# A decoder trunk's feed-forward down stage in seven block products, with the differences on GpSimd

## The chip, the cores and the metric

The kernel runs on one core of a Trainium2 chip. The metric is the device time of one execution in microseconds (us), lower is better; the runs are given by their median. A core has TensorE (PE in the profile), VectorE (DVE), ScalarE (ACT), GpSimd (POOL) and SyncE (SP), which issues most of the transfers here.

## The reference

Two layers of a decoder trunk over 512 tokens of width 1024, all in float32. Each layer has two feed-forward half-steps, one around a token mixer and one after a cross-attention to 256 memory tokens:

```python
def swiglu(x, w_gu, w_down):
    g, u = jnp.split(x @ w_gu, 2, axis=-1)
    return (jax.nn.silu(g) * u) @ w_down

for layer in range(DEPTH):                     # 2
    f = swiglu(rmsnorm(h, g[0]), ffn_w_gu[layer, 0], ffn_w_down[layer, 0])
    h = h + 0.5 * rmsnorm(f, g[1])
    m = mixer(rmsnorm(h, g[2]))                # even: sparse attention and RG-LRU; odd: gated linear attention
    h = h + rmsnorm(m, g[3])
    c = mem_cross_attention(rmsnorm(h, g[4]), rmsnorm(mem, g[6]), ...)
    h = h + rmsnorm(c, g[5])
    f = swiglu(rmsnorm(h, g[7]), ffn_w_gu[layer, 1], ffn_w_down[layer, 1])
    h = h + 0.5 * rmsnorm(f, g[8])
```

The hidden width of the feed-forward parts is 2816, so `w_down` is 2816 x 1024: 22 blocks of 128 rows (k-tiles). The down product is (512 x 2816) times (2816 x 1024), four times in the program.

## The kernel before

**Precision.** Every large product is made of three matmuls. A float32 operand is split into a high part (`ACT.Copy` on ScalarE into the type fp32r, `split_hi`) and the rest (a subtraction on VectorE, `split_lo`); the product sums high x high, high x low and low x high.

**Weights.** All weights stand in memory as one stream of units of 128 x 1024 elements (512 KB). SyncE loads each unit into a raw buffer (`w_raw`, two places; `w_raw_odd`, two more in the feed-forward parts), ScalarE and VectorE split it into one of four slots (`w_hi`, `w_lo`), and TensorE reads it. SyncE waits for the split of the unit that had the raw place before (`w_ready`), ScalarE for the last matmul on the slot (`w_free`). `AHEAD` is 4: in the loop over units, ScalarE and VectorE split unit q + 4 when unit q is done.

**The feed-forward part.** `ffn` has two stages. Gate-up makes 22 hidden tiles of 128 features by 512 tokens; the first two plainly, the other 20 each by a seven-product scheme (`seven`) on blocks of 256 tokens, with its weight sums on VectorE. One such pair of gate and up tiles takes 84 matmuls of 256 columns; ScalarE and VectorE fill `act_raw`, the product of silu(gate) and up. The down stage (`output(i, "down", 11, ...)`) is plain: for each half of the 1024 output columns (`hf`), eleven units of two k-tiles by 512 columns; for each unit, four token tiles `t` accumulate in four banks of PSUM. The activation tiles are stationary (128 x 128), the weights move (512 columns). In the first half, ScalarE and VectorE also split the activations, two k-tiles at a time (`act_upper`, `act_lower`), into `act_hi` and `act_lo`. The last three units of the second half are kept in places of their own and run tile by tile, so that the norms of finished token tiles begin while TensorE works.

**Around it.** `post_square` on ScalarE squares and sums each finished tile from PSUM, `store_half` on VectorE multiplies it by the gain into `f`, `post` and `update` scale it and add it to the residual `h`. Then `norm` scales `h` into `f`, TensorE transposes it (`turn_x`), and ScalarE and VectorE split the transposed tile into `x_hi` and `x_lo`. Each engine runs its list in the written order; semaphores order the engines among each other. GpSimd has work in the even mixer (part 1: a convolution, part of the RG-LRU, six weight splits) and some masks; in the feed-forward parts it has none.

## Time and profile before

| what | value |
|---|---|
| median of 3 runs | 2197.55 us (2197.55 to 2197.93) |
| profiled execution | span 2196.3 us, 1.25 us under the median |
| TensorE busy | 2181.2 us, 99% |
| VectorE busy | 1456.1 us, 66% |
| ScalarE busy | 1127.0 us, 51% |
| GpSimd busy | 110.4 us, 5% |
| mean granted TensorE clock | 0.999 |

The profile is of one execution, by the hardware profiler. The span runs from the first instruction to the last; what the runs' times have beyond it lies around the program. Matmuls are pipelined, so their recorded durations overlap, and the distance from one start to the next is the cost of one. A granted clock of 1.00 is the full 2.4 GHz.

### The profile page before, as it was taken

To read this page: it belongs to the slowest core of one execution; us is meant where nothing else is said; L and a number is where in the kernel's file an instruction comes from. 1 tells how busy PE (TensorE), PEld (TensorE's weight loads), DVE (VectorE), ACT (ScalarE), POOL (GpSimd) and SP (SyncE) were. 2 spreads that over 40 slices of the span, in tenths; PEclk is the share of its full clock that TensorE was granted. 3 is DMA by queue.
4 is the path that set the end of the run, shared out by engine and by line. 5 is a ranking of instruction groups with operands and counts; after the bars stand their busy time and mean duration, and the time that the engine had idled before them with its cause. 6 is when DMAs were issued, how large, how long until landed. Compare 5 with 4: busy or idle time off the path is not lost.

```text
span 2196.3 us, 36637 instructions
## 1 busy us (share of the span) xinstructions
PE 2181.2 (99%) x13844; PEld 1944.0 (89%) x13844; DVE 1456.1 (66%) x2185; ACT 1127.0 (51%) x1881; POOL 110.4 (5%) x104
## 2 busy tenths in 40 slices
PE   9999999999999999999999999999999999999999
PEld 8999888775888899998899998887868889999987
DVE  8888636788666598874388885345266656888732
ACT  6555524476554565563365554245345546555531
POOL 0000000675000000000000000000000000000000
PEclk9999999999999999999999999999999999999999
DMA  4332332221452233332323323322214422333322
GB/s 164 105 105 95 115 106 63 77 77 49 144 165 79 74 115 105 105 105 96 115 87 105 105 95 115 115 81 87 96 36 138 155 79 77 103 105 105 110 99 78
DMA packets 61953, 221.44 MB, mean 101 GB/s; under 512 B 7953, under 2 KB 8081, under 8 KB 61858
## 3 DMA queue, kind: packets, MB, share of 16 engines
q1 hardware_dynamic: 57456, 208.69, 28.9%
q10 hardware_dynamic: 4402, 11.46, 1.5%
q8 instruction: 62, 1.02, 0.2%
q14 instruction: 33, 0.27, 0.0%
HBM read 218.03 MB, written 2.10 MB: 100 GB/s over the span
## 4 chain that ended last, share of the span: by engine, by line
PE 93%; DVE 4%; ACT 1%; POOL 1%; issue 1%; DMA 0%; DVEq 0%; POOLq 0%
PE ps L2099 12%; PE ps L2100 12%; PE ps L2101 12%; PE ps L2195 11%; PE ps L2197 11%; PE ps L2196 11%; PE ps L479 6%; PE ps L480 6%; PE ps L481 6%; PE ps L2035 1%; DVE e_sc L1768 1%; DVE e_max L1767 1%; DVE e_sc L1783 1%; PE ps L2583 0%; PE ps L2560 0%
## 5 line engine op out<-in xcount | busy, mean ns | idle before, releaser
L417 DVE TENSOR_TENSOR w_lo<-w_raw,w_hi 128x1024 fp32r<-128x1024 f32 x204 | 252.5, 1241 | 358.2 <-ACT w_hi L412 357.3
L412 ACT ACTIVATE w_hi<-w_raw 128x1024 fp32r<-128x1024 f32 x210 | 221.6, 1057 | 311.4 <-PE ps L2197 225.4
L2099 PE MATMUL ps<-t_hi,w_hi 128*128 128x256 f32 x1280 | 362.3, 283 | 0.0
L2100 PE MATMUL ps<-t_lo,w_hi 128*128 128x256 f32 x1280 | 362.2, 283 | 0.0
L2101 PE MATMUL ps<-t_hi,w_lo 128*128 128x256 f32 x1280 | 362.2, 283 | 0.0
L2099 PE MATMUL ps<-x_hi,w_hi 128*128 128x256 f32 x960 | 271.7, 283 | 0.0
L2100 PE MATMUL ps<-x_lo,w_hi 128*128 128x256 f32 x960 | 271.7, 283 | 0.0
L2101 PE MATMUL ps<-x_hi,w_lo 128*128 128x256 f32 x960 | 271.7, 283 | 0.0
L1490 DVE TENSOR_TENSOR w_lo<-f,w_hi 128x1024 fp32r<-128x1024 f32 x152 | 186.2, 1225 | 124.0 <-ACT w_hi L840 124.0
L479 PE MATMUL ps<-x_hi,w_hi 128*128 128x256 f32 (+1 forms) x736 | 250.8, 341 | 1.6 <-DVE x_lo L1367 0.9
L480 PE MATMUL ps<-x_lo,w_hi 128*128 128x256 f32 (+1 forms) x736 | 246.0, 334 | 0.0
L481 PE MATMUL ps<-x_hi,w_lo 128*128 128x256 f32 (+1 forms) x736 | 245.8, 334 | 0.0
L2100 PEld LDWEIGHTS ps<-t_lo,w_hi 128*128 128x128 f32 x1280 | 245.7, 192 | 0.0
L2101 PEld LDWEIGHTS ps<-t_hi,w_lo 128*128 128x128 f32 x1280 | 245.7, 192 | 0.0
L2099 PEld LDWEIGHTS ps<-t_hi,w_hi 128*128 128x128 f32 x1280 | 245.7, 192 | 0.0
L2195 PE MATMUL ps<-w_hi,act_hi 128*128 128x512 f32 x608 | 236.6, 389 | 0.0
L2196 PE MATMUL ps<-w_lo,act_hi 128*128 128x512 f32 x608 | 236.6, 389 | 0.0
L2197 PE MATMUL ps<-w_hi,act_lo 128*128 128x512 f32 x608 | 236.5, 389 | 0.0
L853 ACT ACTIVATE tmp<-ps 128x256 f32<-128x256 f32 x320 | 123.1, 385 | 173.9 <-PE ps L2101 171.1
L840 ACT ACTIVATE w_hi<-f 128x1024 fp32r<-128x1024 f32 x152 | 160.4, 1055 | 85.2 <-PE ps L2101 84.4
L2099 PEld LDWEIGHTS ps<-x_hi,w_hi 128*128 128x128 f32 x960 | 184.3, 192 | 0.0
L2100 PEld LDWEIGHTS ps<-x_lo,w_hi 128*128 128x128 f32 x960 | 184.3, 192 | 0.0
(352 smaller groups left out, 4317.8 us busy)
## 6 DMA issues: line engine op xcount, KB each, us to landing
w_raw<-in_wstream SPq DMA_DIRECT2D x310, 512.0 KB, 3.3
w_raw_odd<-in_wstream SPq DMA_DIRECT2D x80, 512.0 KB, 3.3
tmp<-in_post_gains ACTq DMA_DIRECT2D x8, 512.0 KB, 5.1
gain_bc<-in_gains ACTq DMA_DIRECT2D x7, 512.0 KB, 3.8
h<-in_x SPq DMA_DIRECT2D x4, 512.0 KB, 5.7
c_mem<-in_mem ACTq DMA_DIRECT2D x2, 1024.0 KB, 5.8
out_dram<-h SPq DMA_DIRECT2D x3, 512.0 KB, 2.7
c_gain<-in_mem_gains ACTq DMA_DIRECT2D x2, 512.0 KB, 7.5
```

The lines of the kernel that those rows point to most:

```text
L412: nc.scalar.activation(weights(v)[0], raw(v), ACT.Copy).then_inc(w_hi_ready, 1)
L417: nc.vector.tensor_tensor(wl, raw(v), wh.bitcast(f32), ALU.subtract).then_inc(w_ready, 1)
L479: nc.tensor.matmul(dst, wh, xh, start=start, stop=False)
L480: nc.tensor.matmul(dst, wh, xl, start=False, stop=False)
L481: return nc.tensor.matmul(dst, wl, xh, start=False, stop=stop)
L1490: nc.vector.tensor_tensor(wl, S[:, n * UW:(n + 1) * UW], wh.bitcast(f32), ALU.subtract)\
L2099: nc.tensor.matmul(dst, wh[:, at], xh[:, b, :], start=first, stop=False, skip_group_check=True)
L2100: nc.tensor.matmul(dst, wh[:, at], xl[:, b, :], start=False, stop=False, skip_group_check=True)
L2101: last = nc.tensor.matmul(dst, wl[:, at], xh[:, b, :], start=False, stop=final, skip_group_check=True)
L2195: nc.tensor.matmul(dst, ah, wh, start=start, stop=False)
L2196: nc.tensor.matmul(dst, ah, wl, start=False, stop=False)
L2197: return nc.tensor.matmul(dst, al, wh, start=False, stop=stop)
```

## The change

The down stage becomes a seven-product scheme on 2 x 2 blocks. The hidden features are cut in even and odd k-tiles (11 each), the tokens in two halves of 256, the output columns in two halves of 512. Each product takes one block of activations (or a sum of blocks), 11 k-tiles by 256 tokens, and one block of weights (or a sum), 11 k-tiles by 512 columns. A product is run in six steps (`PU`): five of two k-tiles and one of one k-tile; a step is 12 matmuls (the last 6) over two token tiles. There are 42 steps and 42 weight units in a part, where there were 22.

The products run in turn: `LOW_2`, `LOW_1`, `SUM_1`, `SUM_2`, `LOW_3`, `SUM_3`, `SUM_4`. `LOW_` products take a weight block as it is, `SUM_` products a running difference of weight blocks, made on GpSimd (`block_sum`) in place over the block kept since `LOW_1` (in the space of `x_hi` and `x_lo`), or over the raw buffer. The sums of activation blocks (`s3_sum` in gate-up; `second`, `first`, `third` in down) are on GpSimd as well, and two of the gain multiplies (`gained`). ScalarE and VectorE split each step's operand (`op_upper`, `op_lower`, 512 elements) into a ring of nine places and each step's weights as before. ScalarE copies a finished product's banks to `f` where they are needed twice (`keep_tiles`), VectorE adds the other product to it (`down_add`), and `down_square` squares from `f`. Post and update of token tiles 0 and 1, and the scaling of the next norm for them, are placed inside the last product; tiles 2 and 3 follow after it. The last two units are run tile by tile, with the next part's transpositions between.

```diff
+QT = FT // 2
+PU = -(-QT // 2)
+PRODUCTS = 7
+LOW_2, LOW_1, SUM_1, SUM_2, LOW_3, SUM_3, SUM_4 = range(PRODUCTS)
+BLOCK = (1, 0, 2, 3, 3, 0, 1)
+RING = 9
...
-    "ffn": [("gate_up", 2 * FT), ("down", FT)],
+    "ffn": [("gate_up", 2 * FT), ("down", PRODUCTS * PU)],
...
         def split_hi(act, v):
-            act.wait_ge(w_in[RAW[v]], RAW_COUNT[v] * 16)
+            if v in DOWN and DOWN[v][1] in SUMMED:
+                act.wait_ge(down_sum, sum_count(v))
+            else:
+                act.wait_ge(w_in[RAW[v]], RAW_COUNT[v] * 16)
...
+            def ffn(i):
+                n0, s0, d0 = nffn[i] * FT, SEVENS[i], U[i, "down"]
+                q0, r0 = 3 * PU * nffn[i], len(SUMMED) * PU * nffn[i]
+                for k in range(QT):
+                    pool.wait_ge(gu_free, n0 + 2 * k + 3)
+                    place = by_half[:, 0, 1, k, :]
+                    nc.gpsimd.tensor_tensor(place, by_half[:, 0, 0, k, :], place, ALU.subtract).then_inc(s3_sum, 1)
+                def second(m):
+                    pool.wait_ge(gu_free, n0 + 2 * (2 * m + TILES[m] - 1) + 4)
+                    pool.wait_ge(s3_sum, QT * nffn[i] + 2 * m + TILES[m])
+                    nc.gpsimd.tensor_tensor(operand(SUM_2, m), operand(SUM_4, m), operand(SUM_3, m), ALU.subtract)\
+                        .then_inc(op_sum, 1)
+                def first(m):
+                    pool.wait_ge(op_sum, q0 + 2 * m + 1)
+                    pool.wait_ge(op_ready, PRODUCTS * PU * nffn[i] + PU * LOW_1 + m + 1)
+                    nc.gpsimd.tensor_tensor(operand(SUM_1, m), operand(SUM_2, m), operand(LOW_1, m), ALU.add)\
+                        .then_inc(op_sum, 1)
+                def third(m):
+                    pool.wait_ge(op_ready, PRODUCTS * PU * nffn[i] + PU * LOW_2 + m + 1)
+                    nc.gpsimd.tensor_tensor(operand(LOW_3, m), operand(LOW_2, m), operand(SUM_2, m), ALU.subtract)\
+                        .then_inc(op_sum, 1)
+                def block_sum(p, m):
+                    v = d0 + PU * p + m
+                    pool.wait_ge(w_in[RAW[v]], RAW_COUNT[v] * 16)
+                    if p == SUM_3:
+                        pool.wait_ge(down_sum, r0 + PU + m + 1)
+                        nc.gpsimd.tensor_tensor(raw(v), block_place(m), raw(v), ALU.subtract).then_inc(down_sum, 1)
+                    else:
+                        pool.wait_ge(w_ready, d0 + PU * {SUM_1: LOW_1, SUM_2: SUM_1, SUM_4: SUM_2}[p] + m + 1)
+                        if p == SUM_4:
+                            pool.wait_ge(down_sum, r0 + 2 * PU + m + 1)
+                        nc.gpsimd.tensor_tensor(block_place(m), raw(v), block_place(m), ALU.subtract)\
+                            .then_inc(down_sum, 1)
+                def gained(o):
+                    pool.wait_ge(o_sq, square_count(i, o, 1))
+                    pool.wait_ge(post_in, 16 * (i + 1))
+                    place = f[:, 0:2, o * SEQ:(o + 1) * SEQ]
+                    nc.gpsimd.tensor_tensor(place, place, tmp[:, 2 + o:3 + o, :].to_broadcast([P, 2, SEQ]), ALU.mult)\
+                        .then_inc(down_gain, 1)
+                pool.wait_ge(prod, 5 * (s0 + FT))
+                for m in range(PU):
+                    second(m)
+                    first(m)
+                for m in range(PU):
+                    block_sum(SUM_1, m)
+                for m in range(PU):
+                    block_sum(SUM_2, m)
+                for m in range(PU):
+                    third(m)
+                gained(0)
+                for m in range(PU):
+                    block_sum(SUM_3, m)
+                gained(1)
+                for m in range(PU):
+                    block_sum(SUM_4, m)
...
+            def down(i):                                  # ScalarE
...
+                for c in range(last):
+                    if d0 + c + AHEAD < NU:
+                        split_hi(act, d0 + c + AHEAD)
+                    while ahead <= min(c + 6, 2 * c + 5, last - 1):
+                        op_upper(i, ahead)
+                        ahead += 1
...
+                    if c == PU * LOW_3 + PU + 1:
+                        down_square(i, 1, 0)
+                        down_square(i, 1, 1)
...
+            def down(i):                                  # VectorE
+                for c in range(last):
+                    if d0 + c + AHEAD < NU:
+                        split_lo(dve, d0 + c + AHEAD)
+                    while ahead <= min(c + 6, 2 * c + 5, last - 1):
+                        op_lower(i, ahead)
+                        ahead += 1
...
+                    if c == PU * SUM_4:
+                        down_add(i, 0, 2)
+                        down_add(i, 0, 3)
+                        post(i + 1, 0)
+                        update(i + 1, 0)
...
+            def down(i):                                  # TensorE
+                first_bank = (2, 0, 4, 0, 4, 0, 2)
+                def tiles(c, t, final):
+                    p, m = divmod(c, PU)
+                    pe.wait_ge(w_ready, d0 + c + 1)
+                    pe.wait_ge(op_ready, PRODUCTS * PU * nffn[i] + c + 1)
...
+                            nc.tensor.matmul(dst, ah, wh, start=start, stop=False, skip_group_check=True)
+                            nc.tensor.matmul(dst, ah, wl, start=False, stop=False, skip_group_check=True)
+                            last = nc.tensor.matmul(dst, al, wh, start=False, stop=stop, skip_group_check=True)
```

The engine names in comments are added here. Step c of a part is weight unit c of its 42.

## Rows read from the trace of the kernel before

**Rows 1.** The page: engines, and the chain that ended last.

```profile
PE 2181.2 (99%) x13844; PEld 1944.0 (89%) x13844; DVE 1456.1 (66%) x2185; ACT 1127.0 (51%) x1881; POOL 110.4 (5%) x104
...
PE 93%; DVE 4%; ACT 1%; POOL 1%; issue 1%; DMA 0%; DVEq 0%; POOLq 0%
```

**Rows 2.** Windows, the first down stage: stretch, its length, busy time by engine.

```profile
core 0: us, PE busy (x) PEld busy (x) DVE busy (x) ACT busy (x) POOL busy (x), PEclk, DMA share, GB/s
239.50:359.10 119.60, 119.42 (x532) 98.64 (x530) 52.23 (x61) 44.35 (x59) 0.00 (x0) 1.00 0.35 114
```

**Rows 3.** TensorE's timeline in down, 24 matmuls apart: start, duration, instruction.

```profile
246.35 0.39 PE L2195 MATMUL ps<-w_hi,act_hi 128*128 128x512 f32 x1
...
251.79 0.39 PE L2195 MATMUL ps<-w_hi,act_hi 128*128 128x512 f32 x1
```

**Rows 4.** VectorE's timeline in down and after it.

```profile
251.78 1.23 DVE L417 TENSOR_TENSOR w_lo<-w_raw,w_hi 128x1024 fp32r<-128x1024 f32 x1 [3.08 <-ACT w_hi L412]
252.92 1.22 DVE L1598 TENSOR_TENSOR act_lo<-act_raw,act_hi 128x1024 fp32r<-128x1024 f32 x1
...
349.16 1.29 DVE L1338 SCALAR_TENSOR_TENSOR h<-f,stat,h 128x1024 f32<-128x1024 f32 x1
```

**Rows 5.** ScalarE's timeline in down.

```profile
250.69 1.06 ACT L412 ACTIVATE w_hi<-w_raw 128x1024 fp32r<-128x1024 f32 x1 [3.43 <-PE ps L2197]
251.65 1.04 ACT L913 ACTIVATE act_hi<-act_raw 128x1024 fp32r<-128x1024 f32 x1
...
295.50 0.60 ACT L692 ACTIVATE tmp<-ps 128x512 f32<-128x512 f32 x1 [0.24 <-PE ps L2197]
296.00 0.19 ACT L692 ACTIVATION_READ_ACCUMULATOR tmp<-ps 128x1 f32 x1
```

**Rows 6.** GpSimd's timeline in the even mixer.

```profile
439.85 2.36 POOL L614 TENSOR_TENSOR w_lo<-w_raw,w_hi 128x1024 fp32r<-128x1024 f32 x1
...
495.91 1.33 POOL L629 TENSOR_TENSOR tmp<-tmp,e_t 128x512 f32<-128x512 f32 x1
...
506.00 1.30 POOL L647 TENSOR_TENSOR tmp<-e_bd,tmp 128x512 f32<-128x512 f32 x1
507.38 2.15 POOL L648 TENSOR_TENSOR e_xc<-tmp,e_xc 128x512 f32<-128x512 f32 x1
...
516.43 1.30 POOL L647 TENSOR_TENSOR tmp<-gain_bc,tmp 128x512 f32<-128x512 f32 x1
```

**Rows 7.** VectorE's timeline in the same stretch.

```profile
496.13 2.18 DVE L417 TENSOR_TENSOR w_lo<-w_raw,w_hi 128x1024 fp32r<-128x1024 f32 x1
...
506.34 2.04 DVE L417 TENSOR_TENSOR w_lo<-w_raw,w_hi 128x1024 fp32r<-128x1024 f32 x1
508.30 1.77 DVE L1834 SCALAR_TENSOR_TENSOR e_gate<-e_t,e_gate 128x512 f32<-128x512 f32 x1
...
516.72 0.69 DVE L1817 TENSOR_TENSOR x_lo<-ps,x_hi 128x512 fp32r<-128x512 f32 x1 [1.72 <-ACT x_hi L1157]
```

**Rows 8.** TensorE's timeline where the next part's first projection starts.

```profile
361.23 0.39 PE L2197 MATMUL ps<-w_late,act_lo 128*128 128x512 f32 x1
361.46 0.28 PE L479 MATMUL ps<-x_hi,w_hi 128*128 128x256 f32 x1
```

**Rows 9.** VectorE's timeline in the last gate-up pairs; TensorE's matmuls start 0.12 us apart.

```profile
226.68 1.22 DVE L1490 TENSOR_TENSOR w_lo<-f,w_hi 128x1024 fp32r<-128x1024 f32 x1 [0.97 <-ACT w_hi L840]
...
229.29 1.23 DVE L1490 TENSOR_TENSOR w_lo<-f,w_hi 128x1024 fp32r<-128x1024 f32 x1 [0.67 <-ACT w_hi L840]
230.43 0.68 DVE L1496 TENSOR_TENSOR w_lo<-w_raw_odd,w_hi 128x512 fp32r<-128x512 f32 x1
```

**Rows 10.** TensorE's timeline at the end of gate-up: products three and seven of a pair begin.

```profile
232.32 0.28 PE L2099 MATMUL ps<-t_hi,w_hi 128*128 128x256 f32 x1
...
238.08 0.28 PE L2099 MATMUL ps<-t_hi,w_hi 128*128 128x256 f32 x1
```

**Rows 11.** DMA issues: size, median time from issue to landing.

```profile
w_raw<-in_wstream SPq DMA_DIRECT2D x310, 512.0 KB, 3.3
```

**Rows 12.** Windows around the one fall of the clock, and in the odd mixer.

```profile
520.00:524.00 4.00, 2.50 (x10) 1.35 (x10) 3.96 (x6) 4.00 (x9) 3.32 (x4) 1.00 0.00 0
524.00:528.00 4.00, 3.09 (x12) 1.34 (x12) 4.00 (x8) 2.43 (x7) 2.17 (x3) 0.78 0.01 2
...
1600.00:1620.00 20.00, 20.00 (x108) 9.62 (x107) 14.10 (x39) 7.52 (x30) 0.00 (x0) 1.00 0.00 1
```

More of the change, by code:

```diff
@@ L67, in trunk @@
     ALU, ACT, AX = mybir.AluOpType, mybir.ActivationFunctionType, mybir.AxisListType
-    U, _ = unit_starts(parts)
-    NU = wstream.shape[0]
+    U, NU = unit_starts(parts)
     NP = len(parts)
@@ L193, in bank @@
             return ps[:, b, :]
-        w_in = [sem(f"w_in{n}") for n in range(4)]
+        w_in = [sem(f"w_in{n}") for n in range(4 + PU)]
         w_hi_ready = sem("w_hi_ready")
@@ L297, in trunk @@
                         continue
-                    late = q - (k - late_units(i)) if seg in ("down", "out") else -1
+                    if seg == "down" and q >= PRODUCTS * PU - 2:
+                        SLOT.append(SLOTS + q - (PRODUCTS * PU - 2))
+                        LAST_USE.append(u - PU)
+                        continue
+                    late = q - (k - late_units(i)) if seg == "out" else -1
                     if kind == "cross" and seg == "out" and q == k // 2:
@@ L325, in trunk, with width, block_place, unit_source @@
                     RAW_COUNT.append(raw_count[s])
-        def raw(u):
-            return w_raw[:, RAW[u], :] if RAW[u] < 2 else w_raw_odd[:, RAW[u] - 2, :]
+        DOWN = {U[i, "down"] + n: (i, n // PU, n % PU) for i, (kind, _, _) in enumerate(parts) if kind == "ffn"
+                for n in range(PRODUCTS * PU)}
+        TILES = (2,) * (PU - 1) + (QT - 2 * (PU - 1),)
+        def width(u):
+            return TILES[DOWN[u][2]] * SEQ if u in DOWN else UW
+        def raw(u):
+            if RAW[u] >= 4:
+                return block_place(DOWN[u][2])
+            return w_raw[:, RAW[u], 0:width(u)] if RAW[u] < 2 else w_raw_odd[:, RAW[u] - 2, 0:width(u)]
+        def block_place(m):
+            return d_t[:, 2 * m:2 * m + TILES[m], :].rearrange("p a b -> p (a b)")
+        def unit_source(u):
+            return block_place(DOWN[u][2]) if u in DOWN and DOWN[u][1] in (SUM_1, SUM_2, SUM_4) else raw(u)
         def feeds_selection(i):
@@ L354, in trunk, with square_count, half_count, full_count @@
         nffn = [sum(k == "ffn" for k, _, _ in parts[:i]) for i in range(NP)]
+        def square_count(i, o, t):
+            if parts[i][0] == "ffn":
+                return TT * 2 * i + (2 * o + t if t < 2 else 2 + 2 * o + t) + 1
+            return TT * 2 * i + TT * o + t + 1
+        def half_count(i, t):
+            before = sum(2 if parts[k][0] == "ffn" else 1 for k in range(i) if not feeds_selection(k + 1))
+            return before + (2 if parts[i][0] == "ffn" and t >= 2 else 1)
+        def full_count(i, hf, t):
+            return sum(2 * (TT - 1) for k, _, _ in parts[:i] if k != "ffn") + (TT - 1) * hf + t + 1
+        def down_cols(o, t):
+            hf = o if t < 2 else 1 - o
+            return slice(hf * SEQ, (hf + 1) * SEQ)
         ncross = [sum(k == "cross" for k, _, _ in parts[:i]) for i in range(NP)]
@@ L705, in post_mean @@
                 else:
-                    act.wait_ge(half_ssq, sum(not feeds_selection(k) for k in range(1, i + 1)))
-                    act.wait_ge(o_sq, TT * (2 * i - 1) + t + 1)
+                    act.wait_ge(half_ssq, half_count(i - 1, t))
+                    act.wait_ge(o_sq, square_count(i - 1, 1, t))
                     bias = stat[:, i, t:t + 1]
@@ L787, in norm @@
                     whole(1)
+                    whole(2)
+                    upper(3)
+                    whole(3)
+                elif parts[i - 1][0] == "ffn":
+                    down_square(i - 1, 1, 2)
+                    post_mean(i, 2)
+                    down_square(i - 1, 1, 3)
+                    post_mean(i, 3)
+                    whole(0)
+                    square(2)
+                    whole(1, (0,))
+                    square(3)
+                    whole(1, (1,))
+                    upper(2)
                     whole(2)
@@ new lines, in ffn, with op_upper @@
+                down(i)
+            def op_upper(i, c):
+                p, m = divmod(c, PU)
+                if p == LOW_2:
+                    act.wait_ge(gu_free, nffn[i] * FT + 2 * (2 * m + TILES[m] - 1) + 4)
+                elif p in (SUM_1, SUM_2, LOW_3):
+                    done = {SUM_1: 2 * m + 2, SUM_2: 2 * m + 1, LOW_3: 2 * PU + m + 1}[p]
+                    act.wait_ge(op_sum, 3 * PU * nffn[i] + done)
+                elif p == SUM_3:
+                    act.wait_ge(s3_sum, QT * nffn[i] + 2 * m + TILES[m])
+                if c >= RING:
+                    act.wait_ge(w_free, U[i, "down"] + c - RING + 3)
+                nc.scalar.activation(list(operand_place(c))[0], operand(p, m), ACT.Copy).then_inc(op_hi, 1)
@@ L1294, in _ @@
                     gla(i)
-            for t in range(TT):
-                post(NP, t)
+            for t in range(2, TT):
+                down_square(NP - 1, 1, t)
+                post_mean(NP, t)
         @block.vector
@@ L1415, in norm @@
                     return lower
+                elif parts[i - 1][0] == "ffn":
+                    down_add(i - 1, 1, 2)
+                    down_add(i - 1, 1, 3)
+                    post(i, 2)
+                    update(i, 2)
+                    post(i, 3)
+                    update(i, 3)
+                    scale(2)
+                    scale(3)
+                    lower(2)
+                    lower(3)
                 else:
@@ L1434, in last_update @@
             def last_update():
[L1435 to L1437 removed]
+                down_add(NP - 1, 1, 2)
+                down_add(NP - 1, 1, 3)
+                post(NP, 2)
+                update(NP, 2)
                 post(NP, TT - 1)
```

357 lines of the change are left out of this document (261 added, 96 removed).

## The prediction

> **What bounds the kernel now.** The page comes first. TensorE is busy for 99% of the span, and the chain that ended last is 93% TensorE [rows 1]. So only two things can shorten this kernel, fewer or shorter matmuls, and anything can lengthen it that leaves TensorE without operands. Next I read the down stage as a stretch. Between 239.5 and 359.1 TensorE is never starved, VectorE is busy 52.2 of 119.6 us, ScalarE 44.4, GpSimd not at all [rows 2]. TensorE's own timeline gives the cadence: the 24 matmuls of one unit start at 246.35 and those of the next at 251.79, so 5.44 us a unit, 0.2267 us a matmul of 512 columns [rows 3]. The recorded 389 ns are longer than the spacing because matmuls overlap; only the spacing counts. Four feed-forward parts of 22 units make 4 x 119.7 = 479 us. In each unit ScalarE and VectorE split one weight unit and, in the first half, one activation unit: VectorE 1.14 us and ScalarE 0.96 us from start to start for 1024 elements [rows 4, 5].
>
> **What is removed.** Seven products of 11 k-tiles by 2 row tiles, three matmuls each, are 462 matmuls in place of 22 x 8 x 3 = 528. 66 x 0.2267 = 15.0 us less per part, 59.8 us in all; the stage would take 104.7 us. The shape (128x128 stationary, 512 moving) stays, so the cadence stays. That is all the gain there is.
>
> **What is added on VectorE and ScalarE.** A step is now 12 matmuls, 2.72 us, 42 steps a part (35 of two tiles, 7 of one). Each step needs a weight split (1024 elements) and an operand split (512). VectorE: 35 x (1.14 + 0.60) + 7 x (0.60 + 0.34) = 67.5 us; six adds from PSUM (0.6 each), two updates, one gain multiply and two scalings (1.14 to 1.2 each) bring it to about 77 us. ScalarE: 35 x (0.96 + 0.50) + 7 x 0.8 = 57 us and the squares, 0.8 each [rows 4, 5]. Both are under 104.7 us, so neither engine alone would be the bound.
>
> **What is added on GpSimd.** In gate-up eleven differences of 256 elements; in down 18 operand sums (15 of 512 elements, 3 of 256), 24 weight sums (20 of 1024, 4 of 512), two gain multiplies of 1024. Free of VectorE, GpSimd's rows show 2.36 us for 1024 elements and 1.30 for 512 [rows 6]; 256 would be some 0.75 by the same slope. 15 x 1.30 + 3 x 0.75 + 20 x 2.36 + 4 x 1.30 + 2 x 2.36 = 78.9 us. Alone that too fits in 104.7 us.
>
> **Where they do not fit together.** The mixer before has the one stretch where GpSimd and VectorE work side by side, and the two timelines read together are the centre of this forecast [rows 6, 7]. GpSimd starts a 512-element product at 506.00 and ends at 507.30. VectorE starts a weight split at 506.34; it takes 2.04 us in place of 1.22 and ends at 508.38, so its data moved for only 1.07 us, from the moment GpSimd ended. GpSimd's next op starts at 507.38 and takes 2.15 us, that is 1.15 us after 508.38, ending at 509.53. VectorE's next starts at 508.30 and ends at 510.07, 0.54 us after 509.53. At 495.91 and 496.13 the same again (2.18 us). They alternate, strictly, with nothing overlapped. At 516.72 VectorE reads PSUM and SBUF beside a running GpSimd op and takes its normal 0.69: only ops with two SBUF inputs are held. So there is one shared passage, and I sum the time each op holds it: VectorE 1.07 for 1024 elements, 0.54 and 0.27 below; GpSimd 1.15 for 512, 0.6 for 256, and 2.23 for 1024 (between twice 1.15 and 2.36 less the same start-up of 0.15).
>
> The Trainium skill (SBUF — State Buffer, section Who interferes with whom) says the same of a Vector instruction with two SBUF inputs against a GpSimd instruction that reads SBUF, and exempts one with at most one SBUF input. By that rule the six adds from PSUM stay out of the sum; were they in, it would be 3.2 us a part larger. By that rule, the trace agrees.
>
> The holds of one part:
> VectorE, weight splits 35 x 1.07 + 7 x 0.54 = 41.2; operand splits 35 x 0.54 + 7 x 0.27 = 20.8; updates, gain multiply, scalings 5 x 1.07 = 5.4. Together 67.4 us.
> GpSimd, operand sums 15 x 1.15 + 3 x 0.6 = 19.1; weight sums 20 x 2.23 + 4 x 1.15 = 49.2; gain multiplies 4.5. Together 72.8 us.
> Sum 140.2 us, against 104.7 us of matmuls. A full step on a weight sum holds 2.23 + 1.07 + 0.54 = 3.84 us where TensorE takes 2.72: in four of seven products TensorE waits 1.1 us in every step. Before, nothing of GpSimd was in this stage, and VectorE's own 43 us of splits were hidden.
>
> **What is not saturated.** (a) GpSimd is let go at about 238.0, after product five of the last pair, but its second op waits for operand 6, which VectorE makes in loop 1, behind ScalarE's wait for step 1 (239.5 + 5.4). Some 3.4 of those 9 us are lost. (b) Before product SUM_4, GpSimd multiplies the second gain; that waits for two squares, which ScalarE issues after step 31, behind its split of unit 35. Queued behind it on GpSimd is every weight sum of the last product, and behind those ScalarE's split_hi(36) and TensorE. I take 2 us of idle passage; TensorE itself stands some 6 us there. (c) After the last scaling come a transposition and nine matmuls, 0.8 + 2.0 us. From 238.0: 140.2 + 3.4 + 2 + 2.9 = 148.5, so the stage ends at 386.5. Before, the next projection starts at 361.46 [rows 8]. That is +25 us. With the ops' whole durations in place of their holds (VectorE 73, GpSimd 78.9, sum 152) it is +37 us. The rows showed holds, but 44 GpSimd ops and their semaphores will not always follow at once; I take +28, nearer the holds.
>
> The last part has no next norm (two scalings, four splits, two transpositions: 8 us less against 2.3 less before), so +22. 3 x 28 + 22 = +106 us.
>
> **Edits at nothing.** The eleven gate-up differences hold the passage 0.6 us once in two pairs, 20 us. The two sums' splits end at 227.91 and 230.52, and TensorE first reads them at 232.3 and, 24 matmuls of 0.12 us later, 235.2; the last split ends at 231.11 and is read at 238.08 [rows 9, 10]. 4 us of slack cover 0.6; without it the four parts' 44 cost 44 x 0.6 = 26 us. Weight DMA rises from 22 to 38.5 units of 512 KB a part, about 135 GB/s in place of 114 [rows 2]; a load lands in 3.3 us [rows 11], and the loop split, load, sum, split, split is 3.3 + 2.36 + 1.06 + 1.22 us plus waits of at most 3.3, 11.2 us for four units, 2.8 a step, under 3.84. If its waits double, it is 4.4 a step: 22 steps x 0.56 = +12 us a part, the upper end. The norms after the stage lose about a microsecond, since two tiles are scaled inside it as before; gain 0 to 1 us a part, taken as nothing.
>
> **The sum.** Against the profiled span 2196.3: 2302. The runs' median lies 1.25 us above the span, so 2303.5.
>
> **Rivals.**
> Other side: the passage does not bind, because GpSimd runs in gaps that VectorE leaves anyway. For it: each engine alone fits (77 and 79 of 104.7 us). Then the stage shrinks by 15 us less the stand before SUM_4, about 3: 4 x -12 = -48, 2150 us. Against it: every overlap in the mixer was stretched. It decides from the point where holds sum to under 105 us a part; I count 140. 8%.
> The loop through DMA and GpSimd binds instead: +12 a part, 2350. 10%.
> The clock: in 524 to 528, after a stretch in which TensorE was busy 2.5 of 4 us, the granted clock was 0.78, partly its lower level of 1.2 GHz; in 1600 to 1620 it stayed at 1.00 through 108 small matmuls [rows 12]. If it stayed at 1.2 GHz through a stage, a step is 5.44 us, TensorE is the bound again, and 462 matmuls take 209 us: +80 to 90 a part, 2540. I expect it to fall only at the two stands (before SUM_1 and SUM_4), where TensorE then is slower than 3.84 for a step or two and catches up: 0 to 3 us, inside the range. 4%.
> The Trainium skill (TensorE: Matmul & The Clock Gate, Part 1) has the clock at half after idleness and full again after sustained work; that rule, too, would bring it back within the product.
>
> **How the numbers follow.** Forecast 76%, loop 10%, no binding 8%, clock 4%, gain eaten to within 0.2% 2%. Holds alone without (a) and (b) give +20 x 3 + 14 = +74, 2271; whole durations give +142, 2340; the loop 2350. I widen the lower end to 2250, since VectorE's holds may partly fall where GpSimd waits on a semaphore, and take 2250 to 2355. 0.2% of this kernel, 4.4 us, is what a measurement can tell. Faster 8%, same 2%, slower 90%.
>
> **What would show it.** In the changed profile: 1848 down matmuls at 0.227 us; a weight sum on GpSimd of 2.4 us alone and above 3 beside VectorE; operand splits on VectorE of 0.6 stretched to 1.5 to 3; TensorE's waits in down put to VectorE's and ScalarE's splits, most in the four summed products; down stages of about 147 us. The forecast is wrong if VectorE's splits keep 1.22 and 0.68 us, if the stage is under 120 us, or if the clock in it reads well under 1.

## The result, and the profile after it

The changed kernel took 2328.78 us (median; 2328.68 to 2329.37), the kernel before on the same chip 2197.55 us (2197.43 to 2197.93). The ratio is 1.0597, with a 95% interval of 1.0582 to 1.0612: 131.2 us slower. The forecast was 2303.5, +106, with a range of 2250 to 2355. The profiled execution spans 2327.1 us, 130.8 more than before.

From the page of the changed kernel, the lines that answer to [rows 1], and two groups of GpSimd's:

```profile
PE 2179.5 (94%) x13580; PEld 1914.6 (82%) x13580; DVE 1844.4 (79%) x2404; ACT 1252.6 (54%) x2101; POOL 585.6 (25%) x324
...
PE 66%; POOL 13%; DVE 10%; issue 9%; ACT 2%; DMA 0%; POOLq 0%; DVEq 0%; ACTq 0%
...
L767 POOL TENSOR_TENSOR act_raw<-act_raw 128x256 f32<-128x256 f32 x44 | 70.6, 1604 | 1458.0 <-DVE act_raw L1752 735.0 <-DVE act_raw L1819 723.0
```

The chain was 93% TensorE; 23% of it now runs through GpSimd and VectorE. Windows of the first down stage, against the one of [rows 2], and of four short stretches in it:

```profile
core 0: us, PE busy (x) PEld busy (x) DVE busy (x) ACT busy (x) POOL busy (x), PEclk, DMA share, GB/s
238.00:398.00 160.00, 123.74 (x503) 95.95 (x502) 149.57 (x121) 77.80 (x117) 100.97 (x44) 0.93 0.41 134
```

```profile
276.00:280.00 4.00, 4.00 (x12) 3.02 (x12) 4.00 (x2) 1.81 (x3) 4.00 (x2) 0.65 0.39 131
...
364.00:368.00 4.00, 4.00 (x11) 3.13 (x12) 4.00 (x2) 1.86 (x3) 4.00 (x2) 0.57 0.43 131
384.00:388.00 4.00, 0.00 (x0) 0.00 (x0) 3.13 (x6) 3.97 (x7) 0.00 (x0) 0.58 0.26 78
388.00:392.00 4.00, 2.95 (x11) 2.76 (x12) 3.90 (x7) 2.37 (x5) 0.00 (x0) 0.50 0.36 97
```

VectorE was busy 52 of 120 us before; now it is busy 150 of 160. Some 60 us of that is waiting inside its instructions: over the whole program it is busy 239 us longer than in run 1 below, where the same instructions have nothing beside them. The granted clock is below 1.00 behind the longer stands of TensorE (0.65 behind 3.96 us up to 275.76, 0.57 and 0.50 in the rows above), not behind every one: behind 1.67 us up to 281.87 it reads 1.00.

The timelines of GpSimd and VectorE in the stretch of the operand sums, which answer to [rows 6, 7]; GpSimd first:

```profile
253.08 1.62 POOL L778 TENSOR_TENSOR act_raw<-d_s,act_raw 128x512 f32<-128x512 f32 x1
254.66 2.28 POOL L772 TENSOR_TENSOR d_s<-act_raw 128x512 f32<-128x512 f32 x1
257.02 1.62 POOL L778 TENSOR_TENSOR act_raw<-d_s,act_raw 128x512 f32<-128x512 f32 x1
```

```profile
253.48 2.31 DVE L488 TENSOR_TENSOR w_lo<-d_t,w_hi 128x1024 fp32r<-128x1024 f32 x1
255.71 1.78 DVE L1897 TENSOR_TENSOR d_op<-act_raw,d_op 128x512 fp32r<-128x512 f32 x1
257.42 2.31 DVE L488 TENSOR_TENSOR w_lo<-d_t,w_hi 128x1024 fp32r<-128x1024 f32 x1
```

Go through the ends: GpSimd 254.70, VectorE 255.79 (1.09 later), GpSimd 256.94 (1.15 later), VectorE 257.49 (0.55 later), GpSimd 258.64 (1.15 later). They alternate, and the pattern repeats after 3.94 us; the forecast's holds give 1.15 + 1.07 + 1.15 + 0.54 = 3.91. In the weight sums:

```profile
275.63 2.85 DVE L1897 TENSOR_TENSOR d_op<-act_raw,d_op 128x512 fp32r<-128x512 f32 x1
278.40 3.40 DVE L488 TENSOR_TENSOR w_lo<-d_t,w_hi 128x1024 fp32r<-128x1024 f32 x1
281.73 2.88 DVE L1897 TENSOR_TENSOR d_op<-act_raw,d_op 128x512 fp32r<-128x512 f32 x1
```

```profile
274.59 6.14 POOL L797 TENSOR_TENSOR d_t<-w_raw,d_t 128x1024 f32<-128x1024 f32 x2
```

One step with two weight sums beside it takes 6.10 us (275.63 to 281.73); the holds give 2 x 2.23 + 1.07 + 0.54 = 6.07. TensorE has 2.72 us of work in it.

**How far the forecast carries through a stage.** Starts of the first and last down matmuls by line, in the first part:

```profile
L2505 PE MATMUL ps<-w_hi,d_op x148: 389/389/796, 240.4 to 378.9; 128*128 128x512 f32 x148
```

By the forecast's holds, starts and stand, without what comes after step 40, this stretch ends at 238.0 + 3.4 + 2 + (140.2 - 5.9) = 377.7, 137.3 us after 240.4. It took 138.5 us here, and 137.4, 137.8 and 138.8 in the other three parts. So the body of the stage came out within 1.5 us. The timelines say the same in another way: from 238 to 378 VectorE had gaps of 8.3 us and GpSimd of 35.6, but both stood together for only 0.9 us (0.5 to 1.3 in the other parts). The rest did not come out. VectorE and TensorE at the end of the first stage:

```profile
378.01 1.27 DVE L1913 TENSOR_TENSOR f<-f,ps 128x512 f32<-128x512 f32 x2
...
382.69 1.28 DVE L1614 SCALAR_TENSOR_TENSOR h<-f,stat,h 128x1024 f32<-128x1024 f32 x1
384.73 1.23 DVE L488 TENSOR_TENSOR w_lo<-w_raw,w_hi 128x1024 fp32r<-128x1024 f32 x1 [0.76 <-ACT w_hi L483]
385.87 1.22 DVE L1945 TENSOR_TENSOR f<-f,tmp 128x1024 f32<-128x1024 f32 x1
...
387.71 1.28 DVE L1635 SCALAR_TENSOR_TENSOR f<-h,stat,gain_bc 128x1024 f32<-128x1024 f32 x1
388.91 1.22 DVE L488 TENSOR_TENSOR w_lo<-w_raw,w_hi 128x1024 fp32r<-128x1024 f32 x1
...
390.62 1.28 DVE L1635 SCALAR_TENSOR_TENSOR f<-h,stat,gain_bc 128x1024 f32<-128x1024 f32 x1
```

```profile
389.05 1.97 PE L2384 MATMUL ps<-ident,f 128*128 128x128 f32 x8 [9.34 <-DVE f L1635]
...
393.80 0.63 PE L2506 MATMUL ps<-w_late_d,d_op 128*128 128x512 f32 x1
394.23 0.63 PE L2507 MATMUL ps<-w_late_d,d_op 128*128 128x512 f32 x1
394.65 1.14 PE L2384 MATMUL ps<-ident,f 128*128 128x128 f32 x8
...
397.69 0.28 PE L573 MATMUL ps<-x_hi,w_hi 128*128 128x256 f32 x1
```

TensorE stands 9.34 us for the first scaling (L1635), then runs nine closing matmuls 0.43 us apart, at the lower clock, in place of 0.23. GpSimd's last sum ended at 374.94, so nothing in these rows has GpSimd beside it. The next projection starts at 397.69; before it was 361.46 [rows 8], +36.2. From the last full step (378.9) to it are 18.8 us, and 16.0 and 16.4 in the next two parts, where the forecast had 8.8. The projections after the second and third parts start at 1169.6 and 1551.5, before at 1100.8 and 1448.7, so 68.8 and 102.8 us later: the parts cost 36.2, 32.6, 34.0 and, with what is left of the 130.8 between the spans, 28.0 us, where the forecast took 28, 28, 28 and 22.

### The profile page after: what moved, and what is told of

Read it like the earlier page. It is cut to its first block, busy times and chain, and to the rows that moved or that the text cites. A ratio compares the mean times of both kernels' runs of the same rounds, so it can differ in the third digit from the quotient of the medians.

```text
span 2327.1 us, 37283 instructions
## 1 busy us (share of the span) xinstructions
PE 2179.5 (94%) x13580; PEld 1914.6 (82%) x13580; DVE 1844.4 (79%) x2404; ACT 1252.6 (54%) x2101; POOL 585.6 (25%) x324
## 4 chain that ended last, share of the span: by engine, by line
PE 66%; POOL 13%; DVE 10%; issue 9%; ACT 2%; DMA 0%; POOLq 0%; DVEq 0%; ACTq 0%
PE ps L2448 11%; PE ps L2450 11%; PE ps L2449 11%; PE ps L573 5%; POOL d_t L797 5%; PE ps L574 5%; PE ps L575 5%; PE ps L2586 4%; PE ps L2587 4%; PE ps L2588 4%; DVE w_lo L488 2%; POOL act_raw L783 2%; DVE d_op L1897 2%; POOL d_s L772 2%; POOL w_raw L792 1%
## 5 line engine op out<-in xcount | busy, mean ns | idle before, releaser
L767 POOL TENSOR_TENSOR act_raw<-act_raw 128x256 f32<-128x256 f32 x44 | 70.6, 1604 | 1458.0 <-DVE act_raw L1752 735.0
L488 DVE TENSOR_TENSOR w_lo<-w_raw,w_hi 128x1024 fp32r<-128x1024 f32 (+1 forms) x168 | 216.7, 1294 | 171.7 <-ACT w_hi L483 170.9
L2505 PE MATMUL ps<-w_hi,d_op 128*128 128x512 f32 x592 | 251.0, 424 | 102.9 <-DVE w_lo L488 69.8
L483 ACT ACTIVATE w_hi<-w_raw 128x1024 fp32r<-128x1024 f32 (+1 forms) x174 | 180.1, 1036 | 142.1 <-DMA w_raw<-in_wstream 80.9
L2505 PEld LDWEIGHTS ps<-w_hi,d_op 128*128 128x128 f32 x592 | 118.0, 199 | 157.4 <-DVE w_lo L488 95.8
L2506 PE MATMUL ps<-w_lo,d_op 128*128 128x512 f32 x592 | 242.5, 410 | 0.0
L2507 PE MATMUL ps<-w_hi,d_op 128*128 128x512 f32 x592 | 241.6, 408 | 0.0
```

The lines of the kernel that those rows point to most:

```text
L483: nc.scalar.activation(weights(v)[0], unit_source(v), ACT.Copy).then_inc(w_hi_ready, 1)
L488: nc.vector.tensor_tensor(wl, unit_source(v), wh.bitcast(f32), ALU.subtract).then_inc(w_ready, 1)
L2505: nc.tensor.matmul(dst, ah, wh, start=start, stop=False, skip_group_check=True)
L2506: nc.tensor.matmul(dst, ah, wl, start=False, stop=False, skip_group_check=True)
L2507: last = nc.tensor.matmul(dst, al, wh, start=False, stop=stop, skip_group_check=True)
```

## The experiments

| Kernel | us | ratio to before, interval |
|---|---|---|
| nothing on GpSimd in down | 2162.01 | 0.9835 (0.9819 to 0.9852) |
| fills that only write | 2184.09 | 0.9936 (0.9920 to 0.9953) |
| gain multiply last | 2324.30 | 1.0574 (1.0557 to 1.0592) |
| all sums on VectorE | 2204.82 | 1.0032 (1.0021 to 1.0044) |
| weight sums on VectorE | 2239.95 | 1.0193 (1.0178 to 1.0209) |
| operand sums on VectorE | 2302.70 | 1.0477 (1.0461 to 1.0493) |
| changed kernel, end reordered | 2331.95 | 1.0609 (1.0593 to 1.0626) |
| changed kernel, norm chain earlier | 2343.19 | 1.0661 (1.0644 to 1.0679) |
| nothing on GpSimd, chain earlier | 2174.11 | 0.9893 (0.9876 to 0.9909) |
| all on VectorE, chain earlier | 2219.03 | 1.0099 (1.0082 to 1.0116) |
| six operand sums on GpSimd, rest on VectorE, end reordered | 2208.38 | 1.0051 (1.0038 to 1.0065) |
| all on VectorE, end reordered, x splits first | 2209.54 | 1.0053 (1.0039 to 1.0067) |

**1. Is it GpSimd's work at all?** The sums and gain multiplies of down are left out; fills of eight columns stand in their places (for the six `second` sums, of the whole operand), with the same waits.

```diff
-nc.gpsimd.tensor_tensor(block_place(m), raw(v), block_place(m), ALU.subtract)
+nc.gpsimd.memset(block_place(m)[:, 0:8], 0.5)
```

> The sums and gain multiplies of GpSimd in the down stage are left out (a fill of 8 columns, or of the 512-element operand for the six 'second' ops, stands in each one's place, with the same waits and semaphores); everything on the other engines stays. Passage theory: the stage is then bound by TensorE, 104.7 us and a little at the end: the changed kernel's 2328.8 less about 33 us a part, 2190 to 2165, and VectorE's splits read 1.22 and 0.68 us again. Rival (the loop split, load, sum, split through the four raw places and the ring of operands binds): still over 2250, since the loads and the waits stay. Rival (placement at the end of the stage): the stand before the first transposition, 9 us a part, stays in full.

2162.01 us, 3 us under the range of the passage theory: without these operations seven products are 35.7 us faster than eight. 59.8 us of matmuls went; 24 came back although nothing contends. In the first part the steps take 100.0 us from the first matmul to the last full step (339.9), which is their matmuls alone, and then 13.2 us pass to the next projection at 353.07; TensorE stands 4.76 us of them, about half of the 9 that were expected to stay. VectorE's splits, grouped by shape (count, busy time, mean ns, idle time before):

```profile
L488 DVE TENSOR_TENSOR w_lo<-d_t,w_hi 128x1024 fp32r<-128x1024 f32 x76 | 93.0, 1224 | 56.1 <-ACT w_hi L483 56.1
...
L1897 DVE TENSOR_TENSOR d_op<-act_raw,d_op 128x512 fp32r<-128x512 f32 x120 | 81.7, 684 | 0.9 <-ACT d_op L1133 0.9
```

In the changed kernel the same groups have means of 2077 and 1548 ns.

VectorE's chain at the end of the stage, from the last adds to the first scaling, in this run:

```profile
334.43 1.28 DVE L1913 TENSOR_TENSOR f<-f,ps 128x512 f32<-128x512 f32 x2
...
344.13 1.28 DVE L1635 SCALAR_TENSOR_TENSOR f<-h,stat,gain_bc 128x1024 f32<-128x1024 f32 x1
```

From the first start to the last end it takes 10.98 us here, and 10.98 us in the changed kernel too (378.01 to 388.99). So GpSimd does not lengthen this chain. What differs is TensorE: here the chain begins 6.3 us before TensorE's last full step is done (340.7), in the changed kernel 1.7 us before (379.7).

**2. Its time or its reads?** Each operation becomes three fills of its output, a half and two wholes, of about the same total time (0.53 + 0.95 + 0.95 us for 1024 elements); nothing is read and no sum is made.

```diff
-nc.gpsimd.tensor_tensor(block_place(m), raw(v), block_place(m), ALU.subtract)
+filled(block_place(m))   # two fills of halves or wholes, each waited for, and a third
```

> Each sum and gain multiply of GpSimd in down becomes three fills of its output (half, whole, whole), which only write; GpSimd is occupied about 2.5 us for 1024 elements and 1.4 for 512, as long as the sums were alone. The sums are left out. Passage theory (a sum's reads are what VectorE's two-input ops wait for): VectorE's splits keep 1.22 and 0.68 us, and the time is within 15 us of the run with nothing on GpSimd. Rival (GpSimd's own length in the chain of splits is what costs): stays near 2300, whatever VectorE's durations.

2184.09 us, 22 more than run 1, where the theory allowed 15. GpSimd was busy for 501.5 us, and VectorE's instructions kept their durations:

```profile
L490 DVE TENSOR_TENSOR w_lo<-d_t,w_hi 128x1024 fp32r<-128x1024 f32 x76 | 93.0, 1224 | 87.9 <-ACT w_hi L485 87.9
L1907 DVE TENSOR_TENSOR d_op<-act_raw,d_op 128x512 fp32r<-128x512 f32 x120 | 81.8, 684 | 6.2 <-ACT d_op L1143 5.7
```

So GpSimd's own length costs 22 us (2184 less 2162), and its reading beside VectorE 145 us (2329 less 2184). That is the shared passage, isolated. The 22 us lie mostly at the end of the stage: in the first part the steps take 101.2 us in place of 100.0, and from the last full step (341.0) to the next projection (359.26) 18.3 us in place of 13.2, with a stand of 9.68 us. The Trainium skill (SBUF — State Buffer, section Who interferes with whom) says that a Vector instruction with two SBUF inputs contends with a GpSimd instruction that reads SBUF and not with one that only writes it. With that, these two runs agree.

**3. The stand before SUM_4** (term (b) of the forecast).

```diff
-gained(1)
 for m in range(PU):
     block_sum(SUM_4, m)
+gained(1)
```

> One thing moved: GpSimd's second gain multiply, which waits for the squares of product LOW_3, stands behind the weight sums of SUM_4 and no longer in front of them. In the changed kernel GpSimd stands 7.1 us before it and TensorE some 3 to 4 us after it. If the order of GpSimd's list costs as I put it (term b), the passage is used in that stand: 4 to 7 us a part less, 2300 to 2312. If the passage is saturated anyway over the rest of the stage, or the end of the stage waits for VectorE: less than 2 us a part, 2321 to 2329.

2324.30: 4.5 us in all, 1.1 a part on average, as the second theory had it; the first part alone gained 3.5 (next projection at 394.19 in place of 397.69) the others between 1.4 gained and 0.7 lost. In the changed kernel the multiply on GpSimd, and the next split on VectorE, read:

```profile
355.58 2.41 POOL L805 TENSOR_TENSOR f<-f,tmp 128x1024 f32<-128x1024 f32 x1 [7.14 <-ACT tmp L894]
```

```profile
361.47 2.28 DVE L488 TENSOR_TENSOR w_lo<-d_t,w_hi 128x1024 fp32r<-128x1024 f32 x1 [5.74 <-ACT w_hi L483]
```

VectorE did idle 5.74 us, and GpSimd 7.14, but one after the other: GpSimd starts at 355.58, before VectorE's last split ends at 355.73. The passage was not idle. With the multiply moved VectorE has no gap there, and nearly all of the time is found again: the sum of holds is the same.

**4. The sum of holds, checked by moving it.** All sums and gains go to VectorE (run a), only the weight sums (b), only the operand sums (c). A sum of 1024 elements then holds 1.07 us in place of 2.23.

```diff
-pool: second, first, third, block_sum, gained
+dve, in down(): second(c - 1); first(c - 1)                     # a, c
+                third(c - 2 * PU - 4)                           # a, c
+                block_sum((c + PU) // PU, c % PU)               # a, b
+                gained(0) at step 22, gained(1) at step 36      # a
```

Run a:

> All down-stage sums and both gain multiplies on VectorE, in the loop over steps, about two steps before they are needed; GpSimd keeps only the eleven gate-up differences. Passage theory: holds fall from 140 to 102 us a part, but VectorE's whole list becomes about 77 + 20 x 1.14 + 4 x 0.6 + 15 x 0.6 + 3 x 0.34 + 2 x 1.14 = 115 us, over TensorE's 104.7, so the stage is 118 to 125 us plus the stand at the end: 2328.8 less 20 to 28 a part, 2215 to 2250. If GpSimd were a help (two engines better than one): slower than 2329.

Run b:

> The weight sums alone (24 a part) go to VectorE; operand sums and the two gain multiplies stay on GpSimd. Nothing is left out of the computation. On VectorE a weight sum holds the passage 1.07 us in place of 2.23 on GpSimd. Theory of the alternating holds: 140.2 - 20 x 1.16 - 4 x 0.6 = 114.6 us a part, which is 25 us a part less: about 2228 us (2215 to 2245). Rival, the loop through DMA and GpSimd decides: a sum on VectorE shortens the loop by 1 us in four units and costs VectorE 1.2 us a step, so 5 to 10 us a part come back at most: 2290 to 2310. Rival, the length of GpSimd's own ops in the chain of a step is what counts: the sums on VectorE remove all of it for weights, and the time comes near that of the kernel with everything on VectorE, 2205.

Run c:

> The operand sums alone (18 a part) go to VectorE; weight sums and the two gain multiplies stay on GpSimd. Nothing is left out of the computation. Theory of the alternating holds: 140.2 - 15 x 0.61 - 3 x 0.33 = 130 us a part, 10 us a part less, about 2289 us (2280 to 2300). Rival, the operand sums of the start are the delay (they stand ahead of all weight sums on GpSimd's queue): then most of the loss of the first products goes, over 15 us a part, under 2270.

Measured 2204.82, 2239.95 and 2302.70, so 124, 89 and 26 us less than the changed kernel; the holds said 100 for (b) and 40 for (c). The direction and the rank hold; of the size, nine tenths came in (b) and two thirds in (c), which ended 3 us above its range. (a) came out 10 us under its range. There VectorE kept up with TensorE: it was busy 124.4 of 128 us from 238 to 366, no longer stretched, and the steps took 105.1 us (240.2 to 345.3) for 100.0 of matmuls; from there to the next projection (365.77) are 20.5 us. In (b) VectorE was busy 105.3 of 108 us up to 346, so there the holds and VectorE's own list come to nearly the same time, and (b) does not tell them apart.

(b) holds a surprise. GpSimd and VectorE in it:

```profile
293.52 20.67 POOL L805 TENSOR_TENSOR f<-f,tmp 128x1024 f32<-128x1024 f32 x1 [14.02 <-ACT tmp L886]
```

```profile
309.49 0.69 DVE L1889 TENSOR_TENSOR d_op<-act_raw,d_op 128x512 fp32r<-128x512 f32 x1
310.09 1.23 DVE L488 TENSOR_TENSOR w_lo<-w_raw_odd,w_hi 128x1024 fp32r<-128x1024 f32 x1
311.22 0.69 DVE L1889 TENSOR_TENSOR d_op<-act_raw,d_op 128x512 fp32r<-128x512 f32 x1
312.33 2.94 DVE L488 TENSOR_TENSOR w_lo<-w_raw,w_hi 128x1024 fp32r<-128x1024 f32 x1 [0.42 <-ACT w_hi L483]
```

GpSimd's multiply, 2.4 us in the changed kernel, lasts 20.67 us. From 293.59 VectorE's instructions follow without a gap at their free durations; at its first gap, 0.42 us, GpSimd gets in, and VectorE's next takes 2.94. There it is not alternation but exclusion. All eight of (b)'s multiplies lasted 6.4 to 20.7 us. In the other seven VectorE had no gap; their ends fit an entry at its first instruction other than one with two large inputs from SBUF: at 352.83 two adds from PSUM (the multiply ends at 355.16), at 1051.44 an instruction on two elements, which lasts 2.35 us (the multiply ends at 1053.77).

**5. Is the end of the stage a matter of order?** TensorE stands at the end even in run 1 (4.76 us before the first transposition). Three edits: scalings and squares of the next norm ahead of the last weight splits, gain multiply of tiles 2 and 3 behind, transpositions behind the closing matmuls (first below); the whole chain some steps sooner (second); the x splits ahead of the weight splits made in steps 40 and 41, and the gain multiply of tiles 2 and 3 one step later still (third).

```diff
 for c in range(last):
+    if i + 1 < NP and c in (last - 4, last - 3):      # first
+        norm_scale(i + 1, c - (last - 4))
+    if i + 1 < NP and c >= last - 2:                  # third
+        norm_lower(i + 1, c - (last - 2))
     split_lo(dve, d0 + c + AHEAD)
...
-    if c == PU * SUM_4: post(i + 1, 0); update(i + 1, 0)
+    if c == PU * SUM_4 - 2: post(i + 1, 0); update(i + 1, 0)   # second
+    if c == PU * SUM_4 + 1: norm_scale(i + 1, 0); norm_scale(i + 1, 1)
```

First edit on the changed kernel:

> Only the order at the end of the stage is changed: the next norm's two scalings on VectorE and its two squares on ScalarE stand ahead of the last weight splits, the gain multiply of tiles 2 and 3 behind them, and the two transpositions of the next norm behind the matmuls that close the stage, tile by tile. Nothing is left out of the computation. TensorE stands some 9 us a part there in three parts, and runs at the lower clock afterwards. Theory that this chain of VectorE is the term that the forecast made too small: 3 x (5 to 8) us less, 2305 to 2314. Rival, the passage is full up to the end and an order within it gives nothing: within 4 us of 2329.

Second edit on the kernel of run 1, on the changed kernel and on (a):

> As the run without GpSimd sums (2162.0 us; the sums and gain multiplies of the down stage are left out, small fills in their place), with the chain of the next norm sooner: the post scalings and updates two steps earlier (34, 35 in place of 36, 37), the norm's squares and scalings all in step 37 in place of 38 and 39 behind the splits of those steps, the gain multiply of tiles 2 and 3 behind step 40. VectorE has idle time here before step 34. Theory that the stand at the end of a stage comes from the place of that chain, since steps are half as long as before: 3 x (4 to 7) us less, 2141 to 2150. Rival, VectorE has too much work in the last steps whatever the order: within 4 us of 2162.

> The changed kernel with the same earlier chain and nothing left out. The post scaling of step 34 now waits for GpSimd's gain multiply. Theory of the place of the chain: 3 x (4 to 8) us less, 2305 to 2317. Theory that every microsecond of the stage is set by the sum of holds and VectorE's queue, so that an earlier chain only makes the splits later: within 4 us of 2329. Rival, a loss: VectorE waits in step 34 for the gain multiply behind GpSimd's sums, 2335 and above.

> The kernel with all sums and gains on VectorE (2204.8), with the same earlier chain and nothing left out. Theory that VectorE is itself full (busy 9.8 to 10 of every 10 us from 250 to 350), so that an order can give nothing: within 5 us of 2205. Rival, the place of the chain counts here too: 3 x (4 to 8) less, 2181 to 2193, under the kernel before.

First edit on (a), with six operand sums on GpSimd:

> Seven products with all sums and gains of the down stage on VectorE, but for the six first operand sums of a part (GpSimd, at the start), and the end of the stage in the order of the run with only that order changed. Nothing is left out of the computation. VectorE's own sum is some 102 us a part against 104.7 of matmuls. Theory that what is left over 2138 in the kernel with everything on VectorE (2204.8) is mostly the stand of 11 us at the end of each of three stages: 2204.8 less 12 to 25, 2175 to 2195, faster than the kernel before (2197.7). Rival, VectorE is itself the bound all through: within 5 us of 2205.

First and third edit on (a):

> The kernel with all sums and gains on VectorE (2204.8), with the end of the stage in this order and nothing left out: the next norm's squares and scalings ahead of the weight splits of steps 38 and 39, the transpositions behind the closing matmuls, and the x_hi and x_lo splits of the two turned tiles ahead of the weight splits of steps 40 and 41, so that they no longer stand behind a split that waits for a weight load. In the run with the same order but the x splits behind (2208.4), TensorE stood to 367.0 for x_lo, while the transposed tile lay ready from 359.8 and ScalarE waited 3.14 us for a weight load. Theory that this queueing behind a load is what holds the next stage: 3 x (3 to 5) us less than 2208, and some 3 x 1 for the operand sums that are not on GpSimd at the start: 2188 to 2196, just under the kernel before (2197.6). Rival, the loads themselves are late for the next stage's first matmuls, so the wait only moves to w_lo: 2200 to 2208.

None gained: 2331.95 against 2328.78; 2174.11 against 2162.01; 2343.19 against 2328.78; 2219.03, 2208.38 and 2209.54 against 2204.82. In three runs the rival had that: the first edit on the changed kernel (within 4 us), the second on it (2335 and above), the first on (a) (within 5 us). The second edit on run 1 and on (a) came out above everything that was expected, the third 1.5 us above its rival. The second edit lost 12 to 14 us everywhere, even where VectorE has idle time: on the kernel of run 1 the first transposition starts 1.5 us sooner (344.00 against 345.47), but ScalarE then waits 5.00 us for a weight load up to 350.62, x_hi and x_lo stand behind that split, and the next projection starts 4.2 us later (357.27 against 353.07). The chain of waits shows what each edit did with the stand. TensorE's waits in the changed kernel, then with its end reordered:

```profile
PE ps L2505 <- DVE w_lo L488: 69.8, 50, 4.0
PE ps L2505 <- issue: 32.8, 12, 5.4
PE ps L2384 <- DVE f L1635: 27.6, 7, 9.3
```

```profile
PE ps L2505 <- DVE w_lo L488: 62.8, 50, 4.0
PE ps L2505 <- issue: 39.2, 13, 5.4
PE ps L573 <- DVE x_lo L1643: 23.7, 4, 7.9
PE ps L2384 <- DVE f L1635: 7.9, 5, 2.0
```

The 27.6 us on the scaling became 7.9 on it and 23.7 one link further, on x_lo. In the run with six sums on GpSimd the reason for that link shows on ScalarE, a split queued behind a weight load, and on TensorE:

```profile
360.37 1.06 ACT L484 ACTIVATE w_hi<-w_raw 128x1024 fp32r<-128x1024 f32 x1 [3.14 <-DMA w_raw<-in_wstream]
361.33 1.07 ACT L908 ACTIVATE x_hi<-ps 128x512 fp32r<-128x512 f32 x2
```

```profile
367.02 0.55 PE L574 MATMUL ps<-x_hi,w_hi 128*128 128x256 f32 x1 [6.33 <-DVE x_lo L1632]
```

The third edit removed just that, and its trace has TensorE's stands here:

```profile
350.20 0.50 PE L2545 MATMUL ps<-w_late_d,d_op 128*128 128x512 f32 x1 [2.80 <-DVE w_late_d L488]
...
355.20 1.97 PE L2424 MATMUL ps<-ident,f 128*128 128x128 f32 x8 [1.96 <-DVE f L1619]
...
358.11 1.97 PE L2424 MATMUL ps<-ident,f 128*128 128x128 f32 x8 [0.95 <-DVE f L1619]
...
362.80 0.55 PE L573 MATMUL ps<-x_hi,w_hi 128*128 128x256 f32 x1 [2.72 <-DVE x_lo L1627]
...
374.65 1.10 PE L2424 MATMUL ps<-ident,f 128*128 128x128 f32 x8 [3.21 <-DVE f L1619]
```

The next projection starts 4.2 us sooner than in the run with six sums on GpSimd, and the time is the same: the wait is now split over five places, the last of them the norm of tile 2 inside the next part. (This run also has no operand sums on GpSimd and the later gain multiply, so it does not differ from that one by the x splits alone.) None of the orders tried gains. That does not rule out one that would: the third edit was never put together with the second, whose loss on the kernel of run 1 lies at that same queue behind a weight load. What the traces suggest beside it is the sum of dependent work. In the kernel before, the first update ends at 350.5 [rows 4], and TensorE is fed from there to the next projection at 361.46 [rows 8]; in the changed kernel TensorE has only 2 x 9 matmuls, 4 us, left when the same updates begin. Run 1 shows that the chain's own 10.98 us do not come from GpSimd; no run cut the chain's work out, so that it is the cause of the loss is argued, not shown. No version with all its work was faster than the kernel before; the closest, (a), is 0.3% slower.

## Why the forecast held, and where it was off

**Cadence and gain: right.** The matmuls keep 0.23 us where TensorE is fed; 59.8 us less.

**The shared passage: right, and the size of the holds too.** Periods of 3.94 and 6.10 us against 3.91 and 6.07, and 137.4 to 138.8 us for the body of a stage against 137.3. Run 2 shows that it is the reads. That both engines stood together for only about 1 us of a stage fits a passage in use nearly throughout. The rival that the passage does not bind (2150) is what the kernel would be near with GpSimd silent (run 1, 2162). The allowance of 3 us a part for whole durations was not needed there. It covers a part of what the end of the stage cost instead, and that is luck: without its 12 us the forecast would have been 2291.5.

**Term (b): right on the waits, not on the idle passage.** 2 us a part taken; removing the stand gave 1.1 on average. ScalarE's and VectorE's waits before SUM_4 are as described, but VectorE uses the passage while GpSimd stands and GpSimd while VectorE stands, so no idle passage shows there. What fills the place of these 2 us in the 137.3 was not taken apart (the adds from PSUM, 0.6 us each, are work of VectorE that the sum of holds leaves out).

**Term (c), the end of the stage: mis-sized.** This is the step that failed; the range held all the same. "A transposition and nine matmuls, 0.8 + 2.0 us" after the last hold, 8.8 us with the holds of what stands before them (half a split, updates, gain multiply, scalings: 5.9); measured 16.0 to 18.8 in three parts, 7 to 10 more. I had summed holds where the passage is no longer contended and VectorE's queue counts instead. In it stand in a row the small statistics instructions of two updates (0.83 us each) and two scalings (0.6 each), two splits of the next part's weights (1.14 each) and a wait of 0.76, 5.9 us together; then come nine matmuls 0.43 us apart, 1.8 us more than at the full clock, behind a transposition that took 1.6 in place of 0.9. Run 1, with GpSimd silent and a stand half as long, still has 13.2 us for the 8.8, so the term was too small without any contention. Against the excess go the 3 us of allowance. That is 5 to 8 us a part in three parts; with the 6 us of the last part (28.0 for 22), whose own end I did not take apart, it is the 25 us by which the forecast was low.

**The clock: expected at two stands, seen at more.** The granted clock read 0.65, 0.57 and 0.50 in windows behind the stands and was back at 1.00 from 280 to 284 and from 368 to 372, inside the product as forecast; over the execution it was 0.978, against 0.999. At the closing matmuls and the transposition before them its price can be read (1.8 and 0.7 us). Inside the product, where TensorE waits anyway, the runs do not separate it.

**Edits at nothing.** A gate-up difference took 1.60 us beside VectorE, not 0.75, and cost nothing: TensorE was busy for 48.00 of 48 us from 190 to 238 in both kernels. The loop through DMA did not bind: a load of w_raw landed in 3.5 us (d_t in 6.7), and in GpSimd's longest wait for one in the first part, 9.30 us up to 331.83, VectorE worked on and TensorE was fed from 324 to 343. The forecast's upper end for this loop was worked out wrongly: by its own terms twice the waits give (7.9 + 6.6) / 4 = 3.6 us a step, still under 3.84; 4.4 needs the load to take twice as long as well.

## What to carry to other kernels

When work goes to GpSimd beside VectorE, add up how long both hold the passage for instructions with two inputs from SBUF, and compare that sum with the engine that bounds the stage; the two engines' loads taken singly (77 and 79 us here) say nothing. The same sums on VectorE cost 124 us less here, because it needs half the time for the same data. A shorter stage also uncovers the dependent chain at its end: price that chain by VectorE's whole queue from the last split on, statistics and the next stage's splits included, and do not count on reordering: the six reordered kernels here moved the stand and removed none of the time.

## What was not expected of the hardware

Sharing is not always by turns: with VectorE's instructions back to back, one GpSimd multiply of 2.4 us lasted 20.67 us, until VectorE had its first gap, and seven others 6.4 to 15.4 us. That GpSimd came from a long wait does not decide it: in (c) a weight sum that came after 21.13 us of waiting (254.85), in the middle of VectorE's instructions, got its turn, and VectorE's next lasted 2.90 us. What was expected, and was seen: GpSimd instructions that only write (fills) left VectorE's two-input instructions at 1224 and 684 ns while GpSimd was busy for 80.10 of 124 us of the stage. In the changed kernel too VectorE's instructions overlap at their ends, yet GpSimd got its turn each time; what decides between the two stays open.
